# Third buffers for two page quarters of a paged selected-attention loop, and two DMA queues that load whole quarters

## The reference, cut to what matters

```
past_c = cache_cmp[page_table].reshape(Bd, PAST_LEN, 2, KV_HEADS, HEAD_DIM)
...
def gather_sel(idx):
    phys = page_table[bi, jp // bpp] * bpp + jp % bpp
    past = pool[phys, :, :, gi, :]
    ...
o_c, o_s, o_w = nsa_core(q, pos, kc_blk, vc_blk, gather_sel, n_sel_blocks, kw, kw_pos)
return combine_nsa(gates, o_c, o_s, o_w)
```

## Time and profile before

| | |
|---|---|
| median of 3 runs | 1040.93 us (1040.17 to 1042.69) |
| the profiled execution's own time | 1036.34 us |
| its span, first to last instruction | 1034.7 us |
| mean granted clock of TensorE | 0.982 of full speed |
| busy: PE, DVE, ACT, POOL | 965.7, 599.1, 298.2, 70.6 us |
| DMA of the page quarters | 128 issues of 256 KB, half SP, half POOL |
| DMA of the windows | 8 issues of 1024 KB, all SP |

### The profile page before, as it was taken

One profiled execution on the slowest core, in us unless ns is written; L12 is line 12 of the kernel. 1 busy time (PEld: TensorE's weight loads), 2 busy tenths in 40 slices (PEclk: granted clock), 3 DMA queues, 4 the chain that ended last, 5 costly groups with the idle time before them and its releaser, 6 DMA issues.

```text
span 1034.7 us, 17598 instructions
## 1 busy us (share of the span) xinstructions
PE 965.7 (93%) x6530; PEld 600.6 (58%) x6530; DVE 599.1 (58%) x1356; ACT 298.2 (29%) x734; POOL 70.6 (7%) x133
## 2 busy tenths in 40 slices
PE   5999999999977999999999999989899899998997
PEld 3576676667754445566755555665555666655443
DVE  3204997797543645999914222448876667766113
ACT  4310010100143023112124221347776434435012
POOL 0000000000000000000012010310000222120000
PEclk9999999999988999999999999999999999999999
DMA  8543644554361443386522351453002878774202
GB/s 350 184 101 123 174 122 143 172 161 100 107 206 42 104 141 123 92 212 193 181 82 101 104 185 53 162 218 109 40 1 97 312 239 301 278 247 164 103 2 90
DMA packets 48879, 153.03 MB, mean 148 GB/s; under 512 B 9497, under 2 KB 23194, under 8 KB 41882
## 3 DMA queue, kind: packets, MB, share of 16 engines
q1 hardware_dynamic: 43674, 135.13, 40.8%
q0 software_dynamic: 5120, 16.78, 4.7%
HBM read 142.26 MB, written 17.89 MB: 155 GB/s over the span
## 4 chain that ended last, share of the span: by engine, by line
PE 78%; DVE 8%; DMA 6%; issue 4%; ACT 1%; POOLq 1%; SPq 1%; POOL 0%; DVEq 0%; ACTq 0%
PE PS L1275 70%; PE PS L1278 8%; DMA arena<-in_csel 4%; DVE arena L2190 1%; DVE arena L2396 1%; DMA arena<-in_wall 1%; POOLq L589 1%; DMA arena<-in_cmem 1%; DVE arena L2001 1%; POOL arena L590 0%; DVE arena L2033 0%; DVE arena L2034 0%; ACT arena L1188 0%; DVE arena L2401 0%; SPq L589 0%
## 5 line engine op out<-in xcount | busy, mean ns | idle before, releaser
L1275 PE MATMUL PS<-arena 128*32 128x64 f32 (+16 forms) x5436 | 833.3, 376 | 21.7 <-issue 7.4
L1275 PEld LDWEIGHTS PS<-arena 128*128 128x128 f32 (+6 forms) x5436 | 478.2, 148 | 348.1 <-issue 220.7
L1278 PE MATMUL PS<-arena 128*128 128x128 f32 (+3 forms) x1094 | 150.4, 285 | 39.7 <-ACT arena L898 11.0
L1278 PEld LDWEIGHTS PS<-arena 128*128 128x128 f32 (+3 forms) x1094 | 125.1, 146 | 78.0 <-issue 40.2
L2033 DVE TENSOR_TENSOR arena<-arena 128x2048 f32<-128x2048 f32 x32 | 73.2, 2288 | 3.6 <-DMA arena<-in_ccmp 2.4
L2034 DVE TENSOR_TENSOR arena<-arena 128x2048 f32<-128x2048 f32 x32 | 73.1, 2285 | 0.0
L1051 ACT ACTIVATE arena<-arena 128x512 f32<-128x512 f32 (+3 forms) x96 | 53.0, 555 | 30.1 <-DVE arena L2190 30.0
L2190 DVE CUSTOM_DVE_ANT_0 arena<-PS,arena 128x512 f32<-128x512 f32 (+3 forms) x96 | 41.5, 487 | 20.6 <-PE PS L1275 20.6
L590 POOL DMA_DIRECT2D arena<-in_csel x64 | 34.7, 541 | 209.4 <-PE PS L1278 99.2
L2294 DVE TENSOR_TENSOR arena<-arena,PS 128x512 f32<-128x512 f32 x16 | 11.0, 687 | 57.0 <-PE PS L1275 56.9
L2036 DVE TENSOR_TENSOR arena<-arena 128x1024 f32<-128x1024 f32 x32 | 39.0, 1219 | 0.0
(11 more groups left out here) (207 smaller groups left out, 560.9 us busy)
## 6 DMA issues: line engine op xcount, KB each, us to landing
arena<-in_wall SPq DMA_DIRECT2D x19, 2048.0 KB, 9.6
arena<-in_ccmp SPq DMA_DIRECT2D x128, 256.0 KB, 3.7
arena<-in_csel POOLq DMA_DIRECT2D x64, 256.0 KB, 5.6
arena<-in_csel SPq DMA_DIRECT2D x64, 256.0 KB, 5.1
arena<-in_cmem SPq DMA_DIRECT2D x32, 256.0 KB, 6.1
arena<-in_win SPq DMA_DIRECT2D x8, 1024.0 KB, 9.3
out_win_s<-in_win SPq DMA_DIRECT2D x1, 8064.0 KB
x_scratch<-arena SPq DMA_DIRECT2D x1, 2560.0 KB, 9.3
```

Of the source, the lines that this page charges most:

```text
L1275: return nc.tensor.matmul(out, lhsT, rhs, start=start, stop=stop, skip_group_check=True)
L1278: return nc.tensor.transpose(out, in_, ident[0:in_.shape[0], 0:in_.shape[0]])
```

## The change

The page quarters get new places, listed in `PAGES`: three for c = 0, 1 and 2, two for c = 3. The third places of quarters 1 and 2 are columns 0 to 2047 and 2048 to 4095 of the residual stream's region, so `x_back` moves from ahead of the samples to the last turns of SP's loop, and sample 7 does not use those two places. SP's queue now loads whole quarters 0 and 2, POOL's whole quarters 1 and 3; the lists of what each queue loads are written anew, one semaphore counts a quarter's four pages where two counted two each, and the two weight blocks change their order and their waits.

```diff
-        FIRST = [four_pages(a) for a in (at(8192, 2048), at(4096, 2048), shared)]
-        LATER = [[four_pages(at(o, 2048)) for o in quads] for quads in ((10240, 0, 2048), (12288, 14336, 16384))]
+        PAGES = [[four_pages(a) for a in quads] for quads in (
+            (at(8192, 2048), shared, at(4096, 2048)),
+            (at(10240, 2048), arena[:, 0:2048], at(12288, 2048)),
+            (at(0, 2048), arena[:, 2048:4096], at(14336, 2048)),
+            (at(2048, 2048), at(16384, 2048)))]
+        def place(t, c):
+            return 2 if t == NB - 1 and c in (1, 2) else t % len(PAGES[c])
+        def last_in(t, c):
+            return max([s for s in range(t) if place(s, c) == place(t, c)], default=None)
...
-        def quad_load(eng, t, c, pages, loaded):
-            places = 2 if c else 3
-            if t >= places:
-                eng.wait_ge(sa_used, START.sa_used + 6 * (t - places) + c + 2)
-            for s in pages:
+        def quad_load(eng, t, c):
+            last = last_in(t, c)
+            if last is not None:
+                eng.wait_ge(sa_used, START.sa_used + 6 * last + c + 2)
+            for s in range(4):
...
             sp.wait_ge(mem_moved, 1)
-            quad_load(sp, 0, 0, range(2), sa_lo)
-            quad_load(sp, 0, 1, range(2), sa_lo)
+            quad_load(sp, 0, 0)
             sp.wait_ge(cp_took, NB + 1)
-            sp.dma_start(Xf, x_dram).then_inc(x_back, 16)
+            quad_load(sp, 1, 2)
             sp.wait_ge(pa_t, BANKS_OF_P * (UNITS - 2))
-            quad_load(sp, 0, 2, range(2), sa_lo)
+            quad_load(sp, 0, 2)
             sp.wait_ge(pa_t, BANKS_OF_P * (UNITS - 1))
-            quad_load(sp, 0, 3, range(2), sa_lo)
             sp.wait_ge(pa_s, PT * UNITS)
             window(0)
             sp.wait_ge(pa_mix, 6)
-            quad_load(sp, 1, 0, range(2), sa_lo)
+            sp.wait_ge(state_out, 16)
+            quad_load(sp, 1, 0)
             window(1)
-            for t in range(1, NB):
-                for c in range(1, 4):
-                    quad_load(sp, t, c, range(2), sa_lo)
+            quad_load(sp, 2, 0)
+            for t in range(2, NB):
+                if t == NB - 1:
+                    sp.wait_ge(sa_used, START.sa_used + 6 * (NB - 3))
+                    sp.dma_start(Xf, x_dram).then_inc(x_back, 16)
+                quad_load(sp, t, 2)
                 if t + 1 < NB:
-                    if t == 1:
-                        sp.wait_ge(state_out, 16)
-                    quad_load(sp, t + 1, 0, range(2), sa_lo)
-                    window(t + 1)
+                    quad_load(sp, t + 1, 0)
+                window(t)
+            sp.wait_ge(sa_used, START.sa_used + 6 * (NB - 2))
+            load_w(B_OUT1 + 1)
             sp.wait_ge(sa_used, START.sa_used + 6 * (NB - 1))
             load_w(B_OUT1)
-            sp.wait_ge(sa_used, START.sa_used + 6 * (NB - 1) + 2)
-            load_w(B_OUT1 + 1)
...
-            quad_load(pool, 0, 0, range(2, 4), sa_hi)
-            quad_load(pool, 0, 1, range(2, 4), sa_hi)
+            quad_load(pool, 0, 1)
+            pool.wait_ge(cp_took, NB + 1)
+            quad_load(pool, 1, 1)
             pool.wait_ge(pa_t, BANKS_OF_P * (UNITS - 2))
-            quad_load(pool, 0, 2, range(2, 4), sa_hi)
             pool.wait_ge(pa_t, BANKS_OF_P * (UNITS - 1))
-            quad_load(pool, 0, 3, range(2, 4), sa_hi)
+            quad_load(pool, 0, 3)
             pool.wait_ge(pa_mix, 6)
...
+            quad_load(pool, 1, 3)
+            for t in range(2, NB):
+                quad_load(pool, t, 1)
+                quad_load(pool, t, 3)
```

More of the change, by code:

```diff
@@ L365, in four_pages, with times @@
             return a.rearrange("p (s c) -> p s c", s=4)
-        FIRST = [four_pages(a) for a in (at(8192, 2048), at(4096, 2048), shared)]
-        LATER = [[four_pages(at(o, 2048)) for o in quads] for quads in ((10240, 0, 2048), (12288, 14336, 16384))]
+        PAGES = [[four_pages(a) for a in quads] for quads in (
[7 more added lines that the diff above has]
+            return max([s for s in range(t) if place(s, c) == place(t, c)], default=None)
+        def times(t, c):
+            return sum(place(s, c) == place(t, c) for s in range(t + 1))
         def skv(t, c):
-            return LATER[t % 2][c - 1] if c else FIRST[t % 3]
+            return PAGES[c][place(t, c)]
         SWKT = at(18432, 1024).rearrange("p (g c) -> p g c", g=2)
@@ L471, in build @@
         fut_set = sem("future_set")
-        sa_lo = [[sem(f"sa_pages01_{c}_{n}") for n in range(2 if c else 3)] for c in range(4)]
-        sa_hi = [[sem(f"sa_pages23_{c}_{n}") for n in range(2 if c else 3)] for c in range(4)]
+        sa_in = [[sem(f"sa_pages_{c}_{n}") for n in range(len(PAGES[c]))] for c in range(4)]
         (sa_cs, sa_cm, sa_ce, sa_cn, sa_imp, sa_mask, sa_ft, sa_fa, sa_fd, sa_s, sa_m, sa_p,
@@ L581, in build @@
         MCv = [at(29696 + 512 * n, 512).rearrange("p (m c) -> p m c", m=2) for n in range(4)]
-        def quad_load(eng, t, c, pages, loaded):
-            places = 2 if c else 3
-            if t >= places:
-                eng.wait_ge(sa_used, START.sa_used + 6 * (t - places) + c + 2)
-            for s in pages:
+        def quad_load(eng, t, c):
[3 more added lines that the diff above has]
+            for s in range(4):
                 page = eng.value_load(ptab[0:1, NPG * t + 4 * c + s:NPG * t + 4 * c + s + 1], min_val=0, max_val=POOL - 1)
                 eng.dma_start(skv(t, c)[:, s, :], I["csel"][bass.ds(page, 1), :, :].rearrange("a p c -> (a p) c")
-                              ).then_inc(loaded[c][t % places], 16)
+                              ).then_inc(sa_in[c][place(t, c)], 16)
         def sample_phase(front, middle, back):
@@ L856, in _ @@
             pool.wait_ge(sig_done, SILUS)
-            quad_load(pool, 0, 0, range(2, 4), sa_hi)
-            quad_load(pool, 0, 1, range(2, 4), sa_hi)
+            quad_load(pool, 0, 1)
+            pool.wait_ge(cp_took, NB + 1)
+            quad_load(pool, 1, 1)
             pool.wait_ge(pa_t, BANKS_OF_P * (UNITS - 2))
-            quad_load(pool, 0, 2, range(2, 4), sa_hi)
             pool.wait_ge(pa_t, BANKS_OF_P * (UNITS - 1))
-            quad_load(pool, 0, 3, range(2, 4), sa_hi)
+            quad_load(pool, 0, 3)
             pool.wait_ge(pa_mix, 6)
[L864 to L872, removed]
+            pool.wait_ge(state_out, 16)
+            pool.wait_ge(gates_written, 16)
+            quad_load(pool, 1, 3)
+            for t in range(2, NB):
+                quad_load(pool, t, 1)
+                quad_load(pool, t, 3)
         @block.scalar
@@ L1868, in front @@
                         if k % 2 == 0:
-                            places = 2 if k else 3
-                            pe.wait_ge(sa_lo[k // 2][number % places], 32 * (number // places + 1))
-                            pe.wait_ge(sa_hi[k // 2][number % places], 32 * (number // places + 1))
+                            c = k // 2
+                            pe.wait_ge(sa_in[c][place(number, c)], 64 * times(number, c))
                         for q in range(2):
```

## The result

The changed kernel takes 1068.72 us (median of 4 runs, 1063.34 to 1071.11) against 1041.81 us for the kernel before beside it: 2.5% slower, ratio 1.0249 with a 95% interval of 1.0203 to 1.0294. Forecast were 1049.5 us and a range of 1039 to 1058. PE does wait for the late window in each of fronts 2 to 7, as forecast; the loss is three times the size forecast, and outside the range.

What follows compares the result with a forecast made beforehand. PE was taken to bound the kernel, busy 965.7 of 1034.7 us. Late window +7.0, clock +2.7, before b(0) -0.9 made +8.8 on 1036.34; with 4.6 to reach the median, 1049.5 us, range 1039 to 1058.

Steps and rivals of the forecast that it cites:

- What bounds the kernel, and the direction: PE's busy time bounds the span; the window behind quarter 0 comes 2.7 us late at step k = 8, so slower.
- Terms 1, 2 and 4: After b, a sample's value-product start: SP's first page 2.00 us, window 3.75 later, PE resumes 0.13 after landing.
- Term 3, the landing: The window's time from issue on SP's queue to landing: 9.3 us, with 8.9 and 10.5 as ends.
- The clock: PE falling to 1.2 GHz after late-window stalls: two falls taken, +2.7 us, with none and six (8.1 us) as ends.
- "0.5 us at most" for quarter 3: Step k = 6, waiting for quarter 3 from POOL: hidden by the late window, 0.5 us at most if uncovered.
- 7.0 us forecast between b(0) and b(6): Six samples, from first to last of these value-product starts: 120.55 us against 113.50, +7.0 us.
- no later than before, nothing: The weight blocks go out no later than before and the last product waits for DVE: no cost.
- Before b(0): Ahead of sample 0's value products: the 1.28 us wait goes, a 0.39 us DVE wait is next, -0.9 us.
- The window in time: Rival: landing within 6.6 us, so the third places save page waits, -5.4 us, 1035.5 us; chance 0.14.
- the clock falls in every front: Rival: six windows 2.7 us or more late, half clock from k = 8 to b each time, 1059 us; chance 0.14.

Runs made afterwards that it cites:

- The filler: The changed kernel with 32 identity transposes ahead of PE's wait for the window in fronts 2 to 7: 1063.64 us in one run, against the profiled 1069.39.
- the two runs without any such wait: Changed kernel: window first with quarter 3 halved over both queues (1040.7 us); or quarter 3 first, the rest a sample ahead (1041.55 us).
- the one whose loads end before the products: Changed kernel with window(t) ahead of the pages at back(t - 2)'s first count in turns 2 to 6, window(7) a sample early: 1034.87 against 1041.93 us.

## Why the prediction was wrong

**What bounds the kernel, and the direction: right.** The window that stands behind quarter 0 is what PE waits for, six times, at step k = 8, and nowhere else in fronts 2 to 6. Moved late alone, in the kernel before, it makes a loss as large (ratio 1.0276 against 1.0249); moved to the front, in the changed kernel, it takes away three quarters of the loss.

**Terms 1, 2 and 4: right.** Window 2 goes out 5.79 us after b(0), window 3 5.83 us after b(1), where 2.00 + 3.75 = 5.75 stood; PE goes on some 0.15 us after the landing. The later windows went out 5.8 to 6.7 us after b, 1.0 us more in the six together than forecast.

**Term 3, the landing: this step failed.** I took 9.3 us from one row, the window at 806.3, and set 10.5 as the upper end. The six measured 10.6 us on the mean, three of them above 10.5: 6 x 1.3 = 7.9 us of the 21 that are missing between b(0) and b(6). The row was no like case: that window had two pages of SP ahead, this one four, and the median of eight landings taken under another order says nothing of this one. Nor does the reason hold for which the 12.5 us were left out: the window at 857.84 also stood behind eight pages of SP, and landed in 9.9 us. The runs give the parts, as differences between the means of single executions: 5.2 to 5.5 us for the window with nothing ahead, 2.1 us for the four pages ahead, 2.8 us for POOL's quarter 3 beside, 0.3 us for what is behind. Two pages more ahead are half of that 2.1 us, so about 1.05 of the 1.3 us that the row at 806.3 falls short; this is an estimate.

**The clock: right kind, wrong count and price.** I took two falls of 1.35 us, 2.7 us in all, and 8.1 us as the end. The clock fell in five of the six fronts, and from k = 8 to b the six lost 9.0 us over 4.7 us each (with the wait for quarter 3 in front 7 left out), some 1.8 us a fall. In fronts 2, 3, 4 and 6 it fell with waits of 3.45 to 5.58 us, which the late landing had made longer than the 2.0 to 2.7 us forecast; after the 2.79 us of front 5 it stayed up. In front 7 eight transposes still took 1.06 us after the window's wait of 3.22 us (the row at 964.05), and it fell only in the second wait, the one for quarter 3. The filler shows the price directly: 4.63 us in each front without a fall.

**"0.5 us at most" for quarter 3: wrong.** In front 7 it holds PE for another 3.46 us behind the window; its last page took 10.5 us to land. SP's window and a weight block of 2 MB, issued at 953.95, were under way beside it. This first of the two blocks went out 20 us ahead of b(6), where in the kernel before the first went out 3 us behind it, so "no later than before, nothing" overlooked that it now shares the engines with quarter 3; no run separates the two. And with the window in time PE waits for quarter 3 by 1.35 to 2.44 us in fronts 2 to 6, and loses 1.7 us more to the clock in four of them. That was the landing once more: 6.2 us from the earlier trace rows, 7.5 measured.

**The sum.** 7.0 us forecast between b(0) and b(6), plus 7.9 for the landing, 9.0 for the clock, 3.5 for quarter 3 and 1.0 for windows that went out later after b than forecast: 28.4. Of the clock's 9.0 the forecast had 2.7.

**Before b(0): right in its own stretch.** The wait of 1.28 us is gone as said. From the row of 56 records that opens the sample phase to b(0) PE takes 14.73 us (817.29 to 832.02), where it took 16.08 (812.41 to 828.49): 1.35 us won, 0.9 forecast. That b(0) all the same stands 3.5 us later comes from ahead of that row, which itself stands 4.9 us later. This is the prompt's part, where the clock differs between executions: the same 1.93 us of idling that left it alone in the earlier trace rows was followed by half clock in the changed kernel's trace (740 to 741 us). In the run with the window first, with the same early loads, the row stands at 811.07, earlier than in the earlier trace rows; so I don't put the 4.9 us down to the change.

**The rivals.** The window in time needed a landing under 6.6 us. A window with nothing ahead does land in 5.2 to 5.5 us. The estimate from the Trainium skill, "DMA: Bandwidth & Descriptors", section "Anatomy of one DMA — SWDGE (gpsimd) path", is 4.4 us, 0.8 to 1.1 us less, from figures that the page gives for a DMA that GpSimd issues, while SP issues the window; with pages ahead and beside it the trace's 9.2 to 12.2 us are at least twice that estimate. The rival would not have paid as I wrote, either: -5.4 us assumed that page waits turn into time, while the two runs without any such wait won nothing that is certain. The rival "the clock falls in every front" came nearest, at 1059 us, with the landing at 10 us and a clock loss of 8.1; it had 0.14.

## What to carry to other kernels

When a load changes its place in a queue, work out its landing from what will be ahead of it and beside it there; a median of landings under the old order is no substitute, and one late load on a chain that closes each turn is paid in every turn, with the clock's fall on top. Give the load with the least slack the front of the queue and halve the latest one over two queues. Loads that no longer hold the engine may still cost it if they run on into its dense stretch of small instructions: look there for waits without a releaser, and for the packets of the instruction queue ahead of them.

## What the runs showed that was not expected

- The wait that the profile calls "issue" grows with DMA traffic: 6.3 us in the kernel before, 12.5 with useless copies added, 12.3 and 10.6 in the two versions without page waits, 4.1 in the one whose loads end before the products. Of each, 3.0 us stand ahead of the products. The others end 1.3 to 1.8 us after a packet of the instruction queue.
- A 1 MB window with nothing ahead lands in 5.2 to 5.5 us, in the loop 9.2 to 12.2: while those six were under way the engines ran at a DMA share of 0.98 to 1.02 and 337 to 375 GB/s, so the order on the queues decided who came late.
- The length of an idle time alone did not decide whether PE's clock fell: it fell after 2.07 us in the run with the window first, stayed up after the 2.79 us at 918.65 in the changed kernel, and after 1.93 us it fell in one execution and not in another.
